# One gate bank and two branch banks in fn and sc, and a new order of the at stage, in a two-layer hybrid mixer kernel

## The reference, cut to what matters

```python
p = hx @ w_in[l]                  # q, k, v, conformer, short conv, Fourier, 4 gates of 1024
y_attn = windowed_latent_attention(q, k, v, kc, vc, sink)
y_conf, y_sc, y_fn = local_branches(...)
gates = jnp.split(jax.nn.sigmoid(p_gate), 4, axis=-1)
m = gates[0] * (ys[0] @ w_brs[0])
for g, y, w in zip(gates[1:], ys[1:], w_brs[1:]):
    m = m + g * (y @ w)
x = x + gt1 * (m @ w_out)
x = x + gt2 * conv_ffn(modulate(rms_norm(x, g_ffn[l]), sh2, sc2), ...)
```

## Time and profile before

| what | us |
|---|---|
| median of 3 runs (lowest, highest) | 1343.0 (1340.77, 1345.43) |
| the profiled execution, its own time | 1344.04 |
| its span, first to last instruction | 1342.3 |
| PE busy (share) | 1287.8 (96%) |
| PEld / DVE / ACT / POOL busy | 1101.3 / 883.2 / 555.6 / 289.8 |
| mean granted TensorE clock | 0.985 of full speed |
| share of PE in the chain that ended last | 78% |

### The profile page before, as it was taken

How to read it: one execution, slowest core, us unless ns; L and a number is a source line. 1 busy time by engine, 2 the same in 40 slices (tenths; PEclk the granted TensorE clock), 3 DMA queues, 4 the chain that set the end, 5 groups by cost and what they waited for, 6 DMA issues and landing times.

```text
span 1342.3 us, 19885 instructions
## 1 busy us (share of the span) xinstructions
PE 1287.8 (96%) x7677; PEld 1101.3 (82%) x7677; DVE 883.2 (66%) x1193; ACT 555.6 (41%) x868; POOL 289.8 (22%) x246
## 2 busy tenths in 40 slices
PE   7999999999999999999999999989999998999997
PEld 1788877777788788787788888889888898999997
DVE  1686378753689568997656664576677466764654
ACT  2322345654333234333123332344566464653543
POOL 0000499310223100112001110002782230120210
PEclk9899999999999999999999999989999999999999
DMA  9364221222546323667456663425333554564560
GB/s 371 112 188 153 81 76 61 71 63 63 161 141 247 107 82 121 202 195 223 140 166 193 196 204 122 151 79 173 119 118 98 169 174 142 172 214 147 181 211 32
DMA packets 51234, 198.75 MB, mean 148 GB/s; under 512 B 5584, under 2 KB 6864, under 8 KB 50896
## 3 DMA queue, kind: packets, MB, share of 16 engines
q1 hardware_dynamic: 51152, 197.62, 45.2%
HBM read 196.55 MB, written 1.05 MB: 147 GB/s over the span
## 4 chain that ended last, share of the span: by engine, by line
PE 78%; DVE 13%; issue 4%; ACT 3%; DMA 1%; SPq 0%; DVEq 0%; ACTq 0%
PE psA L480 22%; PE psA L482 22%; PE psA L481 22%; DVE w_lo L1165 3%; DVE ada_sum L1186 2%; DVE acc L1374 2%; PE psB L480 2%; PE psB L481 2%; PE psB L482 2%; ACT w_hi L881 1%; DMA ada_first<-w_ada 1%; PE psA L501 1%; DVE small L1387 1%; PE psB L726 1%; PE psB L633 1%
## 5 line engine op out<-in xcount | busy, mean ns | idle before, releaser
L480 PE MATMUL psA<-h_hi,w_hi 128*128 128x256 f32 (+1 forms) x1568 | 529.8, 338 | 9.5 <-DVE h_lo L1280 6.4
L481 PE MATMUL psA<-h_lo,w_hi 128*128 128x256 f32 (+1 forms) x1568 | 523.4, 334 | 0.0
L482 PE MATMUL psA<-h_hi,w_lo 128*128 128x256 f32 (+1 forms) x1568 | 523.3, 334 | 0.0
L881 ACT ACTIVATE w_hi<-raw 128x1024 fp32r<-128x1024 f32 (+2 forms) x244 | 277.1, 1138 | 340.3 <-PE psA L482 243.8
L1165 DVE TENSOR_TENSOR w_lo<-raw,w_hi 128x1024 fp32r<-128x1024 f32 (+2 forms) x244 | 332.7, 1364 | 126.7 <-ACT w_hi L881 126.5
L480 PEld LDWEIGHTS psA<-h_hi,w_hi 128*128 128x128 f32 x1568 | 302.6, 193 | 38.5 <-issue 7.6
L481 PEld LDWEIGHTS psA<-h_lo,w_hi 128*128 128x128 f32 x1568 | 302.7, 193 | 28.1 <-issue 0.5
L482 PEld LDWEIGHTS psA<-h_hi,w_lo 128*128 128x128 f32 x1568 | 302.2, 193 | 28.0
L469 POOL TENSOR_TENSOR hid_lo<-sig,hid_hi 128x512 f32 (+3 forms) x44 | 67.7, 1538 | 486.7 <-ACT hid_hi L1129 486.7
L1186 DVE SCALAR_TENSOR_TENSOR ada_sum<-raw,csil,ada_sum 128x1024 f32<-128x1024 f32 x112 | 159.3, 1452 | 0.0
L480 PE MATMUL psA<-hid_hi,w_hi 128*128 128x256 f32 (+1 forms) x352 | 117.8, 335 | 3.5 <-DVE sig L1565 2.1
(11 more groups left out here) (170 smaller groups left out, 1453.9 us busy)
## 6 DMA issues: line engine op xcount, KB each, us to landing
raw<-w_up SPq DMA_DIRECT2D x88, 512.0 KB, 4.2
raw<-w_ada SPq DMA_DIRECT2D x80, 512.0 KB, 3.6
raw<-w_dn SPq DMA_DIRECT2D x32, 704.0 KB, 5.2
raw<-w_in SPq DMA_DIRECT2D x36, 512.0 KB, 4.3
raw<-w_at SPq DMA_DIRECT2D x24, 512.0 KB, 3.5
raw<-w_fn SPq DMA_DIRECT2D x16, 640.0 KB, 3.9
raw<-w_sc SPq DMA_DIRECT2D x16, 640.0 KB, 3.9
raw<-w_cf SPq DMA_DIRECT2D x16, 640.0 KB, 4.0
```

The source lines that it names most:

```text
L480: pe.matmul(out, w0, hi, start=first, stop=False)
L481: pe.matmul(out, w0, lo, start=False, stop=False)
L482: return pe.matmul(out, w1, hi, start=False, stop=last)
L881: act.activation(w_hi[:, s, 0:tiles * P], raw[:, r, 0:tiles * P], ACT.Copy).then_inc(head_done, 1)
```

## The change

In `fn` and `sc` the gate product has one bank (psA0 in layer 0, psA2 in layer 1) and the branch product two (psB3 and psA1, or psB3 and psA3). So a gate product now waits for the tanh of the step before (`sigd`), and a branch product only for the multiplication of two steps before. On DVE the multiplication stands ahead of the exponential sums. The `at` steps run in the order AT_ORDER, with the weights reordered to match; the gates of groups 1 and 3 go to the space of `q`. The layer norm's steps and the ada steps move by one or two steps. The core of the diff:

```diff
-ADA_START = {2: START["in"] + 2, 3: START["at"] + 3, 4: START["at"] + 11}
+ADA_START = {2: START["in"] + 2, 3: START["at"] + 5, 4: START["at"] + 13}
...
-REDUCE = {START["out"] + 3 if _g == 4 else ADA_START[_g] + 10: _g for _g in ADA_START}
+REDUCE = {START["out"] + 4 if _g == 4 else ADA_START[_g] + 10: _g for _g in ADA_START}
...
+AT_ORDER = [(0, 0), (0, 1), (1, 0), (1, 1), (0, 2), (2, 0), (2, 1), (1, 2), (3, 0), (3, 1), (2, 2), (3, 2)]
...
-        def gate_bank(layer, n):
-            return psA[2 * layer + n % 2]
+        def gate_bank(layer, n, name):
+            return psA[2 * layer + n % 2 * (name == "cf")]
+
+        def mix_bank(layer, n, name):
+            return psB[n % 2] if name == "cf" else psA[2 * layer + 1] if n % 2 else psB[3]
...
+                        sp.wait_ge(evac, START["at"] + LEN["at"])
...
-                    if idx == 0:
-                        pe.wait_ge(sigd, 34 * layer + 2)
-                    else:
-                        pe.wait_ge(evac, st.n - 1)
-                    merge(st, y_hi[:, 0:2, :], y_lo[:, 0:2, :], 2, idx, mix_bank,
-                          [(fn_rest, fc0 + 2 * streams(layer)), (evac, st.n)])
+                    pe.wait_ge(sigd, 34 * layer + 2 + idx)
+                    merge(st, "fn", y_hi[:, 0:2, :], y_lo[:, 0:2, :], 2, idx,
+                          [(fn_rest, fc0 + 2 * streams(layer)), (evac, st.n - 1)])
...
-                    pe.wait_ge(evac, st.n - 1)
-                    merge(st, y_hi[:, 2:4, :], y_lo[:, 2:4, :], 2, 8 + idx, mix_bank,
-                          [(sc_rest, 2 * layer + 2), (evac, st.n)])
+                    pe.wait_ge(sigd, 34 * layer + 2 + 8 + idx)
+                    merge(st, "sc", y_hi[:, 2:4, :], y_lo[:, 2:4, :], 2, 8 + idx,
+                          [(sc_rest, 2 * layer + 2), (evac, st.n - 1)])
...
-                    group, part = divmod(idx, 3)
+                    group, part = AT_ORDER[idx]
...
-                        if k is not None and k < len(un):
-                            weight_sum(k)
                         dve.wait_ge(sigd, 34 * layer + 2 + 8 * b + o + 1)
                         dve.wait_ge(chunk_done, st.n + 1)
...
                         dve.scalar_tensor_tensor(t, sg, 1.0, ps, ALU.add, ALU.mult).then_inc(evac, 1)
+                        if k is not None and k < len(un):
+                            weight_sum(k)
...
-                    if idx == 10:
+                    if idx == 11:
                         for c in range(2):
                             dve.wait_ge(ln_head, 2 * layer + c + 1)
```

More of the change, by code:

```diff
@@ L225, in program @@
         sig = [at(f"sig{b}", [NT], F32, t_off + 4 * NT * (2 + b)) for b in range(2)]
+        qsig = [q[:, b, :] for b in range(2)]
         gtmp = [at(f"gtmp{b}", [NT], F32, sum_off + 4 * NT * b) for b in range(2)]
@@ L452, in _ @@
                     add(n0 + START["sc"], idx, idx, gtmp[idx % 2])
-                for idx in range(2, LEN["at"], 3):
+                for group in range(4):
                     for half in range(2):
-                        add(n0 + START["at"], idx, idx // 3 * 2 + half, (gtmp if idx == 2 else tmp)[half])
+                        add(n0 + START["at"], 3 * group + 2, 2 * group + half, (gtmp if group == 0 else tmp)[half])
                 for idx in range(LEN["cf"]):
@@ L740, in attend, with merge @@
                         turns(k - 1)
-                def merge(st, hi, lo, tiles, place, mix, wait):
+                def merge(st, name, hi, lo, tiles, place, wait):
                     pe.wait_ge(rest_done, st.n + 1)
                     reduce_in_front(st)
-                    from_h(st, T, gate_bank(layer, st.n)[:, 0:T]).then_inc(gated, 1)
+                    from_h(st, T, gate_bank(layer, st.n, name)[:, 0:T]).then_inc(gated, 1)
                     reduction_read(st)
@@ L751, in merge @@
                     for c in range(tiles):
-                        mm = product(mix[:, 0:T], st, KD + c, hi[:, c, 0:T], lo[:, c, 0:T],
+                        mm = product(mix_bank(layer, st.n, name)[:, 0:T], st, KD + c, hi[:, c, 0:T], lo[:, c, 0:T],
                                      c == 0, c == tiles - 1)
@@ L775, in _ @@
                         if group == 0:
-                            pe.wait_ge(evac, st.n - 1)
+                            pe.wait_ge(sigd, 34 * layer + 18)
+                            pe.wait_ge(evac, m0 - 1 + part)
                         elif group == 1:
@@ L779, in _ @@
                         else:
-                            pe.wait_ge(evac, m0 + 3 * (group - 1))
+                            pe.wait_ge(sigd, 34 * layer + 18 + 2 * (group - 2) + part + 1)
                         out = pair_bank(layer, group, part)[:, 0:T]
@@ L818, in _ @@
                     st = Step(n0 + START["cf"] + idx, idx)
+                    if idx < 2:
+                        pe.wait_ge(sigd, 34 * layer + 18 + 8)
                     pe.wait_ge(evac, m0 + 9 if idx < 2 else st.n - 1)
-                    merge(st, yc_hi, yc_lo, 2, None, psB[st.n % 2], [(ln_rest, 2 * layer + 2)])
+                    merge(st, "cf", yc_hi, yc_lo, 2, None, [(ln_rest, 2 * layer + 2)])
                 def project(st):
@@ L1078, in _ @@
                         act.wait_ge(chunk_done, st.n + 1)
[L1079 to L1082, removed]
+                        act.wait_ge(evac, m0 - 1 + part if group == 0 else m0 + 3 * (group - 1))
+                        sg = (gsig, qsig, sig, qsig)[group][part]
                         act.activation(sg[:, 0:T], pair_bank(layer, group, part)[:, 0:T], ACT.Tanh, scale=0.5)\
@@ L1430, in step @@
                         sg = (sig if b == 3 else gsig)[st.n % 2][:, 0:T]
-                        ps = (psB[st.n % 2] if b == 3 else mix_bank)[:, 0:T]
+                        ps = mix_bank(layer, st.n, name)[:, 0:T]
                         if b == 0:
@@ L1482, in _ @@
                     if layer == 0:
-                        if idx == 3:
+                        if idx == 5:
                             dve.wait_ge(m_sum, 10)
@@ L1686 @@
             arrays[f"w_{name}{layer}"] = chunks(np.concatenate([gates[b], br[b]], axis=1))
-        at_chunks = []
-        for o in range(0, KD, 2):
-            at_chunks += [gates[0][o], gates[0][o + 1], np.concatenate([br[0][o], br[0][o + 1]])]
+        at_chunks = [gates[0][2 * g + part] if part < 2 else np.concatenate([br[0][2 * g], br[0][2 * g + 1]])
+                     for g, part in AT_ORDER]
         arrays[f"w_at{layer}"] = chunks(np.stack(at_chunks))
```

18 lines of the change are left out of this document (10 added, 8 removed).

## The result

The changed kernel takes 1348.16 us (median of 16 runs, 1344.53 to 1352.89) against 1344.47 for the kernel before in the same sessions: ratio 1.0028, 95% interval 1.0018 to 1.0038. It is a little slower, by some 3.7 us; the forecast was 3. (The 1346 of the forecast stands on the 1343.0 of the first three runs; on 1344.47 the same +3 gives 1347.5.) Beneath that sum two terms of more than 6 us work against each other.

The account below looks back on a forecast made before the run. PE, busy 1287.8 of 1342.3 us, was taken as the bound, so only its idle time could pay. Terms +4.4 + 0.7 - 9.9 + 6.6 + 0.4 = +2.2, say +3, on 1343.0 gave 1346; range 1338 to 1351.5.

Parts of the forecast that it names:

- Layer 1, fn and sc: +4.4: Layer 1, fn and sc: a new loop through ACT's tanh makes a pair of steps 11.8 us, costing 4.4 us.
- its bound of 6: Layer 1, fn and sc: upper bound of 6 us, if 2.5 us idle before place 4's gate lowers the clock.
- Layer 0, fn and sc: +0.7: Layer 0, fn and sc: multiplication delays exponential sums by 0.6 us, mostly hidden; costs 0.7 us, bounds 0 and 4.8.
- The at stage gives 9.9: At stage: two gate products ahead of each branch product remove issue waits, gaining 6.1 us in layer 0, 3.8 in layer 1.
- the moved fold and reduction: Fold and reduction one or two steps later, costed at nothing: DVE does a cf step in some 6.3 us, PE in 6.9.
- The at stage takes 6.6 in layer 0, 0.4 in layer 1: End of at: PE waits for yc_lo, 4.9 us plus 1.7 at low clock in layer 0, 0.4 in layer 1.
- The chain of fifteen pieces: Layer 0 at stage: DVE's work in order from 362.5, 32.1 us in all, leaves yc_lo ready at 394.6.
- The sum: Whole kernel: all terms together +2.2 us, said as +3 with semaphore delays, so the median would be 1346.
- The 0.8 us added for semaphore delays: Whole kernel: delays of 0.1 us in front of some eight gates, taking the sum from +2.2 to +3.
- the signs: Profile after: tanh waits of about 1 us at layer 1's even places, first at gate 4 to 5 us later, among others.
- the chain of ACT and DVE: Layer 1, fn: closed chain of 11.8 us per pair of steps against some 10.6 for PE; removing bank waits doesn't shorten it.

## Why the prediction was right, point by point

**Layer 1, fn and sc: +4.4; measured +7.2.** The mechanism is the one named, and the kernel with the old banks shows it: PE's gate behind the tanh, the tanh behind copy and division. Place 4's gate was put 19.8 us after the first scores (970.8 - 951.02) and started after 19.72. From place 8 on a pair takes 11.82, forecast 11.8. The first two pairs from place 4 on were taken at the steady price and cost 2.6 more: 1.5 for the gate at low clock, which stood only among the bounds (there for an idle time of 2.5 us; it was 2.31); 0.4 and 0.3 between the first exponential and the end of the tanh (5.17 and 5.03 us for 4.73), where ACT waits for DVE's sums; 0.26 where the exponential of the second pair waits for DVE's maxima. ACT's timeline at places 4 and 6:

```profile
980.24 1.34 ACT L1014 ACTIVATE prob<-prob,small 128x512 f32<-128x512 f32 x2 [0.56 <-DVE small L1406]
...
990.40 0.69 ACT L1004 ACTIVATE prob<-psA,small 128x512 f32<-128x512 f32 x1 [0.20 <-DVE small L1395]
...
992.67 1.34 ACT L1014 ACTIVATE prob<-prob,small 128x512 f32<-128x512 f32 x2 [0.73 <-DVE small L1406]
```

With these the term is 6.9 to 7.0; its bound of 6 was too near. This is the piece of the sum that was mis-sized.

**Layer 0, fn and sc: +0.7; measured +0.66**, with the wait at L721 growing from 0.9 to 1.5 us as the term says. It lies inside the scatter of 1.9 us, so the agreement is partly luck; that it is no 4 us is shown by the kernel with the sums first.

**The at stage gives 9.9.** With `yc_lo` early, layer 0 from the last turns to the first `out` product is 6.6 us shorter than before (forecast 6.1), layer 1's at stage 3.8 (38.42 for 42.19; forecast 3.8). Right, and the runs without the new order say 10.5 (7.9 to 13.1 by the two intervals). In layer 0 part of the nearness is luck: PE is at the first `cf` product 6.0 us earlier than before and waits 0.5 there, and the 1.1 us that `cf` then takes less come from the 1.62 us wait at the first `out` product, which is gone, less part of a new wait of 0.9. That wait is there in all five kernels with the old at order and in none with the new one. The prediction looked at no row there and put the moved fold and reduction at nothing; which of the at stage's edits removed the wait was not tested.

**The at stage takes 6.6 in layer 0, 0.4 in layer 1.** Between the changed kernel and the one with `yc_lo` early lie 6.9 us in layer 0 and 0.7 in layer 1. Its two pieces were off in opposite directions: the wait is 6.2 and not 4.9, the low clock cost 1.2 and not 1.7. The chain of fifteen pieces, counted at 32.1 us, took 33.1 (362.22 to 395.33), and the whole difference is `yc_lo` itself, counted at 1.25 us, which took 2.35 beside POOL's additions.

**The sum.** By the marks up to layer 1's first `out` product, without "between", the change costs 5.2 us; the forecast for them was 2.2, and nearly all of the difference is the low clock and the late sums in layer 1's first two pairs. The runs say 3.7 (2.4 to 5.1). The nearness of 1346 to the measured median therefore owes something to luck: the mechanisms and the terms of layer 0 and of the at stage came out near their size (the first of them within its scatter), and layer 1's was 2.8 us too small. The 0.8 us added for semaphore delays had no ground of its own: the loop already counted 0.1 us from the tanh to PE, and it is 0.06. Of the signs, the waits for the tanh are about 1 us only from place 8 on, and the first `at` gate of layer 1 comes 7.1 us later and not 4 to 5.

**Where the prediction was blind.** It treated the chain of ACT and DVE as given ("taking away the bank wait doesn't shorten that chain"), which is right, and didn't ask what in it could be put in another order. The division, 1.34 us that nobody needs until the turns of the next place, stood ahead of a copy and a tanh that PE and DVE wait for; this was worth 6 us in the kernel before and 14 in the changed one.

## What to carry to other kernels

A second buffer helps only if the wait for the buffer is what closes the loop: here bank waits were slack in a chain through one in-order engine, and moving them from one bank to another moved the wait to a worse instruction. Before trading buffers, list what an in-order engine does ahead of the instruction that frees them, and put last what is needed last. When work is reordered on one engine, look on the others for the small operand at the end of a queue: two instructions of 0.6 us, behind a modulation step that nobody waited for, ate a gain of 6 us.

## What the runs showed of the hardware

The same idle time lowers TensorE's clock in one kernel and not in another. In layer 0's at stage PE idles 2.73 us in front of the group 2 product both before the change (first row; its window is in the earlier trace rows) and in the kernel before with the division moved, whose row and window follow:

```profile
366.86 0.62 PE L480 MATMUL psB<-y_hi,w_hi 128*128 128x512 f32 x1 [2.73 <-issue]
```

```profile
368.12 0.47 PE L480 MATMUL psB<-y_hi,w_hi 128*128 128x512 f32 x1 [2.73 <-issue]
```

```profile
368.00:370.00 2.00, 1.88 (x8) 1.61 (x9) 1.00 (x1) 0.97 (x2) 0.00 (x0) 1.00 0.53 218
```

Its clock stays at 1.00 where it was 0.50, and the at stage takes 74.73 us for 76.32. In layer 1 it is the reverse: PE idles 2.31 us in both (the first row and window are the kernel before's, the second those of the one with the division moved), and there the clock falls in the second:

```profile
1068.39 0.36 PE L480 MATMUL psB<-y_hi,w_hi 128*128 128x256 f32 x1 [2.31 <-issue]
```

```profile
1070.00:1072.00 2.00, 2.00 (x19) 2.00 (x18) 0.90 (x3) 0.40 (x1) 0.00 (x0) 1.00 0.33 49
```

```profile
1062.02 0.36 PE L480 MATMUL psB<-y_hi,w_hi 128*128 128x256 f32 x1 [2.31 <-issue]
```

```profile
1064.00:1066.00 2.00, 2.00 (x11) 2.00 (x11) 0.12 (x1) 0.00 (x0) 0.00 (x0) 0.50 0.44 77
```

Five kernels have the old at order, and each has these two waits, of 2.73 and 2.31 us. The clock fell behind five of the ten: in layer 0 in three kernels (the at stage takes 76.1 to 76.3 us against 74.7 in the other two), in layer 1 in two (43.67 against 42.2). So an idle time of 2.3 to 2.7 us carries a price of 1.4 to 1.6 us that may or may not be paid. Each kernel has one profiled execution, so whether the edit ahead of the wait or the execution decides it is not shown. The Trainium skill, "TensorE: Matmul & The Clock Gate", section "Part 1: The HAM clock gate", says that the monitor behind the clock runs free and doesn't reset when a kernel starts. These rows fit that, and none of the runs shows it directly. At place 4 of layer 1, however, all four profiled executions with a single gate bank and the division ahead (the changed kernel, the old at order, the sums first, `yc_lo` early) fell to the low clock at the same gate, behind waits of 2.10 us at place 2 and 2.31 at place 4. The kernel before has one wait of 2.32 us near there and stays at 1.00; that it is the pair of waits that does it was not tested.

The second is that DVE's work runs longer beside POOL's: `yc_lo`, two subtractions of 512 columns, took 2.35 us beside POOL's additions and 1.28 without them, and the prediction had it at its price without them.
